# Ten instead of five groups of modulation weights beside the first projection, six instead of eleven in attention

## The chip, the cores and the metric

One core of one Trainium2 chip runs the whole kernel. The metric is the device time of one execution in microseconds (us). Three executions of the kernel before took 3576.84, 3581.84 and 3585.43 us, median 3581.84 us.

## What is computed

Two transformer blocks in a row on 256 tokens of width 2048. The edit lies in the first block, whose modulation vector is a matrix-vector product with a matrix of 2048 x 12288:

```python
mod = jax.nn.silu(c) @ w_ada[l] + b_ada[l]
shift_m, scale_m, gate_m, shift_f, scale_f, gate_f = jnp.split(mod, 6, axis=-1)
h = modulate(rms_norm(x, pre_norm_mix[l]), shift_m, scale_m)
... = jnp.split(h @ w_in[l], split_at, axis=-1)
o_n, o_m = nsa_mixer(...), moba_mixer(...)
o = jnp.concatenate([o_n, o_m], axis=-1) @ w_o[l]
x = x + gate_m[:, None, :] * rms_norm(o, post_norm_mix[l])
```

shift_m and scale_m are needed before `h @ w_in`; gate_m, shift_f, scale_f and gate_f only after `@ w_o`. The first two are a third of the columns of `w_ada`.

## The kernel before

**Groups and steps.** Every large matrix is streamed from memory in groups of 512 columns (GC) and steps of 512 rows (four k-tiles of 128, STEP_K), so one step is one load of 1 MiB. For a projection (`kind` "lin") a step goes through a ring of four slots `raw`: SyncE loads it (L495), ScalarE copies it to `wH` (L568), VectorE subtracts to get `wL` (`split`, L941), and TensorE multiplies with both (L1687 in `layer`, L1645 in `layer_t`), 48 matmuls of 128x256 a step in `layer`. `wH` and `wL` have two buffers: the split of step l waits until TensorE has ended step l-2. `step_done` counts the ended steps.

**Modulation groups.** `w_ada` has 24 groups. A group is not multiplied on TensorE but summed on VectorE: `ada_step` runs four operations of 128x512 for each of its four steps (L1082 for the first two of a group, L1086 for the others) into two partial sums, counted by `ada_sum`. Then `ada_total` on TensorE adds over the partitions with matmuls against a column of ones (L1608, 16 records a group) and counts `ada_rows`; it waits until all 16 operations of its group are counted.

**Where they run.** Groups 0 to 7 run ahead of everything (`ada_a`), through `raw`. Then comes the projection `w_in` with 11 groups of four steps. Beside it run SIDE = 5 groups through a store of their own, `side` (four slots of 1 MiB) with the sums in `side_acc`: SyncE issues a side load (L502) directly behind the raw load of the same step, in each second group of `w_in` (r == 1), after the old contents of the slot were summed. On VectorE `layer` calls `beside_w_in` behind each split from group 1 on; it does the four sums at steps (r, s) = (1,2), (1,3), (2,0), (2,1). On TensorE `ada_total` follows step (2,2). `w_in` runs as one group ahead of a loop (`over_groups` with first = 1) and five turns of two groups, r = 1 and 2; only SyncE's program counts from r = 0 (first = 0).

**The attention stage.** The remaining 11 groups (`ada_b`) go through `raw` again, which is free between the last step of `w_in` and the first of `w_o`. VectorE sums one before the rotary embedding, one before the compressed scores, and then ADA_BESIDE[b] groups in turn b of the loop over eight score blocks: `mask_max(b + 1)` (L1177 or L1183 first), `weights_of(b)`, the ada groups, and the low half of an output (L1224) where a block ends one. TensorE's program for turn b is the scores of b+1 (L1775, L1780, L1783), the totals of the turn before, the transposes of b (they wait for GpSimd's L1529), and the values of b. The loads of `w_o` are issued when all modulation groups are summed (`ada_sum`); ahead of the first split of `w_o` VectorE computes the modulation and its coefficients (L1228 to L1233).

## Time and profile before

| | |
|---|---|
| median of three runs | 3581.84 us |
| the profiled execution | 3579.93 us |
| its span, first to last instruction | 3577.8 us |
| TensorE matmul busy | 3175.6 us, 89% |
| VectorE busy | 1757.8 us, 49% |
| ScalarE busy | 1277.1 us, 36% |
| mean granted clock of TensorE | 0.921 |
| read from memory | 581.99 MB, mean 164 GB/s |

All times of the trace are microseconds from the first instruction. The granted clock is TensorE's, as a share of 2.4 GHz; 0.50 is 1.2 GHz. Matmuls overlap, so the duration of one record (0.28 us for 256 columns) is more than its distance to the next (0.12 us at full clock). In brackets behind a timeline row stands the idle time of the engine just before it and what ended it.

### The profile page before, as it was taken

Reading aid. Unit: us, or ns where it says so; the run is one execution under the profiler, and the core shown is the slowest. Engines: PE = TensorE matmul, PEld = TensorE weight load, DVE = VectorE, ACT = ScalarE, POOL = GpSimd, SP = SyncE. Lnnn points to the kernel's source line nnn. Section 1 sums busy time; section 2 is a strip of 40 time slices with the busy share of each in tenths; the row PEclk is TensorE's granted clock in tenths of the full one; section 3 lists DMA queues with packets and bytes.
Section 4 is the critical chain, followed back from the end, with each engine's and each line's share of the span. In section 5 each row is a group of like instructions: output and inputs, shape, how many; then the busy total and the mean of one; then the engine's idle time right before and its main releaser. Section 6 shows DMA issues by size and latency. Waiting matters only on the chain.

```text
span 3577.8 us, 49987 instructions
## 1 busy us (share of the span) xinstructions
PE 3175.6 (89%) x20990; PEld 2895.5 (81%) x20990; DVE 1757.8 (49%) x1499; ACT 1277.1 (36%) x1117; POOL 139.0 (4%) x105
## 2 busy tenths in 40 slices
PE   3699866989999999899976777799999899999998
PEld 3699655779888997699965666699997798889977
DVE  7655779454443444544335554234364544434444
ACT  1333122344433443333342332144333444334433
POOL 0000201000000000000003222000000000000000
PEclk6799876989999999999978887799999999999999
DMA  9777456645555555545510000255554455555553
GB/s 368 245 266 269 155 205 218 209 132 178 175 188 177 182 172 180 169 157 184 181 53 7 3 3 0 83 182 182 191 179 159 133 184 176 187 175 179 176 179 127
DMA packets 298809, 587.98 MB, mean 164 GB/s; under 512 B 11840, under 2 KB 17472, under 8 KB 298432
## 3 DMA queue, kind: packets, MB, share of 16 engines
q1 hardware_dynamic: 296176, 581.87, 49.0%
q10 hardware_dynamic: 2512, 4.36, 0.5%
q8 instruction: 93, 1.52, 0.2%
q14 instruction: 28, 0.23, 0.0%
HBM read 581.99 MB, written 4.19 MB: 164 GB/s over the span
## 4 chain that ended last, share of the span: by engine, by line
PE 82%; DVE 9%; ACT 3%; issue 3%; DMA 2%; POOL 0%; SPq 0%; DVEq 0%; ACTq 0%
PE ps L1687 44%; PE ps L1645 25%; PE ps L1917 3%; DMA raw<-w_ada 2%; PE ps L2074 2%; DVE ada_acc L1086 1%; DVE wL L941 1%; ACT wH L568 1%; PE ps L1961 1%; PE ps L1950 1%; DVE sq L1039 0%; PE ps L1713 0%; PE ps L1952 0%; PE ps L1738 0%; PE ps L1967 0%
## 5 line engine op out<-in xcount | busy, mean ns | idle before, releaser
L941 DVE TENSOR_TENSOR wL<-raw,wH 128x2048 fp32r<-128x2048 f32 x448 | 1026.6, 2292 | 1428.8 <-ACT wH L568 1424.0
L568 ACT ACTIVATE wH<-raw 128x2048 fp32r<-128x2048 f32 x448 | 857.4, 1914 | 1585.8 <-PE ps L1687 903.1
L1687 PE MATMUL ps<-actH,wH 128*128 128x256 f32 x4352 | 1240.5, 285 | 65.0 <-DVE wL L941 40.8
L1687 PE MATMUL ps<-actL,wH 128*128 128x256 f32 x4352 | 1238.3, 285 | 0.0
L1687 PE MATMUL ps<-actH,wL 128*128 128x256 f32 x4352 | 1237.9, 284 | 0.0
L1687 PEld LDWEIGHTS ps<-actH,wH 128*128 128x128 f32 x4352 | 842.7, 194 | 68.9 <-issue 55.1
L1687 PEld LDWEIGHTS ps<-actL,wH 128*128 128x128 f32 x4352 | 843.0, 194 | 0.0
L1687 PEld LDWEIGHTS ps<-actH,wL 128*128 128x128 f32 x4352 | 842.5, 194 | 0.0
L1645 PE MATMUL ps<-wH,hidH 128*128 128x512 f32 x1024 | 409.2, 400 | 13.0 <-ACT hid_sq L608 11.9
L1645 PE MATMUL ps<-wL,hidH 128*128 128x512 f32 x1024 | 407.6, 398 | 0.0
L1645 PE MATMUL ps<-wH,hidL 128*128 128x512 f32 x1024 | 407.6, 398 | 0.0
L1645 PEld LDWEIGHTS ps<-wH,hidH 128*128 128x128 f32 x1024 | 194.0, 189 | 62.2 <-ACT hid_sq L608 12.7
L1645 PEld LDWEIGHTS ps<-wL,hidH 128*128 128x128 f32 x1024 | 194.1, 190 | 47.5 <-issue 0.5
L1645 PEld LDWEIGHTS ps<-wH,hidL 128*128 128x128 f32 x1024 | 193.9, 189 | 47.4
L1086 DVE SCALAR_TENSOR_TENSOR ada_acc<-raw,csig,ada_acc 128x512 f32<-128x512 f32 x266 | 190.3, 782 | 4.6 <-DMA raw<-w_ada 4.6
L1645 PE MATMUL ps<-wH,actH 128*128 128x512 f32 x256 | 103.3, 403 | 17.4 <-DVE wL L941 17.4
L1608 PE MATMUL ps<-common,ada_acc 128*128 128x1 f32 x304 | 51.1, 298 | 57.8 <-DVE ada_acc L1086 57.7
L1645 PE MATMUL ps<-wL,actH 128*128 128x512 f32 x256 | 101.8, 398 | 0.0
L1645 PE MATMUL ps<-wH,actL 128*128 128x512 f32 x256 | 101.5, 397 | 0.0
L1608 PEld LDWEIGHTS ps<-common,ada_acc 128*128 128x128 f32 x304 | 50.8, 259 | 60.7 <-issue 52.1
L2074 PE MATMUL ps<-yH,wH 128*128 128x256 f32 x256 | 73.6, 288 | 6.9 <-DVE wL L941 6.9
L2074 PE MATMUL ps<-yL,wH 128*128 128x256 f32 x256 | 73.3, 286 | 0.0
(354 smaller groups left out, 2647.0 us busy)
## 6 DMA issues: line engine op xcount, KB each, us to landing
raw<-w_in SPq DMA_DIRECT2D x96, 1024.0 KB, 5.1
raw<-w_ada SPq DMA_DIRECT2D x76, 1024.0 KB, 6.9
raw<-w_up SPq DMA_DIRECT2D x64, 1024.0 KB, 5.2
raw<-w_down SPq DMA_DIRECT2D x64, 1024.0 KB, 5.1
raw<-w_mlp_up SPq DMA_DIRECT2D x64, 1024.0 KB, 5.3
raw<-w_mlp_down SPq DMA_DIRECT2D x64, 1024.0 KB, 5.1
raw<-w_gates SPq DMA_DIRECT2D x48, 1024.0 KB, 5.2
side<-w_ada SPq DMA_DIRECT2D x20, 1024.0 KB, 7.4
```

The lines of the kernel that those rows point to most:

```text
L568: nc.scalar.activation(wH[:, s % SPLIT if L[name]["spg"] > 1 else r % SPLIT, :, :], raw[:, slot, :, :], ACT.Copy).then_inc(wh_ready, 1)
L941: nc.vector.tensor_tensor(wL[:, b, :, :], raw[:, slot, :, :], wH[:, b, :, :].bitcast(F32), ALU.subtract).then_inc(wl_ready, 1)
L1086: ins = nc.vector.scalar_tensor_tensor(sums[:, n % 2, :], w[:, k, :], csig[:, n:n + 1], sums[:, n % 2, :], ALU.mult, ALU.add)
L1608: ins = nc.tensor.matmul(ps[:, bank, bass.ds(n + g * GT + i * (GT * per), 1)], sums[:, j, n * P:(n + 1) * P], ones[:, 0:1], start=(n == 0 ...
L1645: ins = nc.tensor.matmul(ps[:, acc(name, r) + t, :], v[:, kk, ts], w[:, b, k, :], start=(kk == 0 and j == 0), stop=(kk == STEP_K * spg - 1 ...
L1687: ins = nc.tensor.matmul(out, w[:, b, k, cols], v[:, kk, :], start=(kk == 0 and j == 0 and n % 2 == 0), stop=(kk == STEP_K * spg - 1 and j ...
L1917: ins = nc.tensor.matmul(ps[:, out + f, m % 4 * P:(m % 4 + 1) * P], lhs[:, m, :], rhs_[:, m, :], start=(m % 4 == 0), stop=True, skip_group ...
L1950: nc.tensor.matmul(out, AR[hh][:, j, t, 0, :], ST[:, j, hh * RHEAD:(hh + 1) * RHEAD], start=(h == 0), stop=False, skip_group_check=True)
L1961: ins = nc.tensor.matmul(ps[:, 1, h * RHEAD:(h + 1) * RHEAD], Ym[:, 2 * h + t, :], rhs[:, h * RHEAD:(h + 1) * RHEAD], start=(h == 0), stop ...
L2074: ins = nc.tensor.matmul(out, w[:, b, k, cols], v[:, k0 + k, :], start=(start and k == 0 and j == 0 and m % 2 == 0), stop=(stop and k == S ...
```

## The change

SIDE becomes 10. SyncE's program for `w_in` takes the same shape as the others (first = 1), and a side load follows every raw load from group 1 on. VectorE sums step s of side group r-1 directly behind the split of step s of group r, in both groups of a turn, and waits for the total of the side group before at s = 0. TensorE's total comes behind step 2 of every group from group 1 on. In the attention stage ADA_BEFORE stays (1, 1) and ADA_BESIDE becomes (1, 0, 1, 0, 1, 0, 1, 0), so that `ada_b` has six groups.

```diff
--- before.py
+++ after.py
@@ -39,7 +39,7 @@
 GC = 512
 GT = GC // P
 RAW, SPLIT = 4, 2
-SIDE = 5
+SIDE = 10
 
 
 CMP_LEN, CMP_STRIDE = 32, 16
@@ -455,7 +455,7 @@
         out_of = [g for g, n in ((0, 3), (1, 3), (2, 1), (3, 1)) for _ in range(n)]
         NSUB = len(subs)
 
-        ADA_BEFORE, ADA_BESIDE = (1, 1), (2, 1, 1, 1, 1, 1, 1, 1)
+        ADA_BEFORE, ADA_BESIDE = (1, 1), (1, 0, 1, 0, 1, 0, 1, 0)
         assert len(ADA_BESIDE) == NSUB and sum(ADA_BEFORE + ADA_BESIDE) == 16 - SIDE
         rope_pairs = [QN, QN + 2, QN + 4, QN + 6, KC, KS, KW] + list(range(QM, VM, 2))
         v_pairs = [VS, VW] + list(range(VM, PROJ1, 2))
@@ -495,19 +495,19 @@
                         sp.dma_start(raw[:, slot, :, :],
                                      w[:, k0 + s * STEP_K:k0 + (s + 1) * STEP_K, bass.ds(n0 + r * GC + i * (U * GC), GC)]
                                      ).then_inc(raw_in[slot], 16)
-                        if name == "w_in" and r == 1:
-
-                            side_g = L["ada_a"]["groups"]
-                            sp.wait_ge(ada_sum, STEP_K * (4 * side_g + s + 1) + i * (4 * STEP_K))
+                        if name == "w_in" and not (isinstance(i, int) and r == 0):
+
+                            side_g = L["ada_a"]["groups"] + r - 1
+                            sp.wait_ge(ada_sum, STEP_K * (4 * side_g + s + 1) + i * (8 * STEP_K))
                             sp.dma_start(side[:, s, :, :], w_ada[:, s * STEP_K:(s + 1) * STEP_K,
-                                                                 bass.ds(side_g * GC + i * GC, GC)]).then_inc(side_in[s], 16)
+                                                                 bass.ds(side_g * GC + i * (2 * GC), GC)]).then_inc(side_in[s], 16)
 
                 if l["kind"] == "ada":
                     if l["l0"]:
                         sp.wait_ge(wl_ready, RAW + l["l0"])
                 elif l["a0"]:
                     sp.wait_ge(ada_sum, STEP_K * (RAW + l["a0"]))
-                over_groups(sp, name, 0, body)
+                over_groups(sp, name, int(name == "w_in"), body)
 
             stream("ada_a")
             sp.dma_start(c1[:, :], a["c1"]).then_inc(c1_in, 16)
@@ -1096,14 +1096,11 @@
 
             def beside_w_in(i, r, s):
 
-                s_ = 4 * (r - 1) + s - 2
-                if not 0 <= s_ < 4:
-                    return
-                g = L["ada_a"]["groups"]
-                if s_ == 0:
-                    dve.wait_ge(ada_rows, 2 + g + i)
-                dve.wait_ge(side_in[s_], 16 + i * 16)
-                ada_step(g, s_, side[:, s_, :, :], side_acc, i, 1)
+                g = L["ada_a"]["groups"] + r - 1
+                if s == 0:
+                    dve.wait_ge(ada_rows, 2 + g + i * 2)
+                dve.wait_ge(side_in[s], 16 * r + i * 32)
+                ada_step(g, s, side[:, s, :, :], side_acc, i, 2)
 
             def ada_raw(g):
 
@@ -1688,8 +1685,8 @@
                                                            start=(kk == 0 and j == 0 and n % 2 == 0),
                                                            stop=(kk == STEP_K * spg - 1 and j == 2), skip_group_check=True)
                         ins.then_inc(step_done, 1)
-                        if name == "w_in" and r == 2 and s == 2:
-                            ada_total(L["ada_a"]["groups"], i, 1, side_acc, 6)
+                        if name == "w_in" and not (isinstance(i, int) and r == 0) and s == 2:
+                            ada_total(L["ada_a"]["groups"] + r - 1, i, 2, side_acc, 6)
                         if turn is not None and isinstance(i, int) and i == 0 and r == 0 and s == 0:
                             turned(turn, ((2, 0), (2, 1), (3, 0), (3, 1)))
```

## Rows read from the trace of the kernel before

**Rows 1.** The page: chain that ended last, by line

```profile
PE ps L1687 44%; PE ps L1645 25%; PE ps L1917 3%; DMA raw<-w_ada 2%; PE ps L2074 2%; DVE ada_acc L1086 1%; DVE wL L941 1%; ACT wH L568 1%; PE ps L1961 1%; PE ps L1950 1%; DVE sq L1039 0%; PE ps L1713 0%; PE ps L1952 0%; PE ps L1738 0%; PE ps L1967 0%
```

**Rows 2.** Windows: us; busy (count) per engine; PEclk, DMA share, GB/s

```profile
126.00:391.00 265.00, 264.78 (x2192) 264.81 (x2193) 149.53 (x126) 89.52 (x52) 0.00 (x0) 0.99 0.72 248
223.00:246.00 23.00, 23.00 (x195) 23.00 (x194) 12.81 (x10) 8.43 (x5) 0.00 (x0) 1.00 1.02 364
541.00:592.00 51.00, 34.89 (x170) 29.59 (x169) 46.72 (x77) 13.98 (x46) 7.39 (x6) 0.67 0.69 250
```

**Rows 3.** Chain in order of time, first projection: start, us, what

```profile
192.25 1.68 PE ps L1608 x16
193.93 46.18 PE ps L1687 x384
```

**Rows 4.** Timeline in w_in, VectorE, ScalarE, TensorE: start, us, what [idle before]

```profile
171.20 2.29 DVE L941 TENSOR_TENSOR wL<-raw,wH 128x2048 fp32r<-128x2048 f32 x1 [0.82 <-ACT wH L568]
173.40 2.73 DVE L1086 SCALAR_TENSOR_TENSOR side_acc<-side,csig,side_acc 128x512 f32<-128x512 f32 x4
...
169.25 1.92 ACT L568 ACTIVATE wH<-raw 128x2048 fp32r<-128x2048 f32 x1 [3.85 <-PE ps L1687]
175.01 1.91 ACT L568 ACTIVATE wH<-raw 128x2048 fp32r<-128x2048 f32 x1 [3.84 <-PE ps L1687]
192.29 1.91 ACT L568 ACTIVATE wH<-raw 128x2048 fp32r<-128x2048 f32 x1 [3.85 <-PE ps L1687]
199.83 1.91 ACT L568 ACTIVATE wH<-raw 128x2048 fp32r<-128x2048 f32 x1 [5.63 <-PE ps L1687]
...
192.09 1.84 PE L1608 MATMUL ps<-common,side_acc 128*128 128x1 f32 x16
```

**Rows 5.** TensorE timeline at stops, then windows around them and 500 us

```profile
942.88 0.50 PE L1645 MATMUL ps<-wH,hidH 128*128 128x512 f32 x1 [2.97 <-ACT hid_sq L608]
...
1532.51 0.39 PE L1687 MATMUL ps<-actH,wH 128*128 128x256 f32 x1 [2.01 <-DVE actL L1047]
...
1128.40:1131.70 3.30, 3.30 (x18) 3.30 (x17) 0.55 (x1) 0.00 (x0) 0.00 (x0) 0.51 0.45 99
1533.30:1536.60 3.30, 3.30 (x30) 3.30 (x29) 3.08 (x4) 2.54 (x2) 0.00 (x0) 1.00 0.00 0
3377.80:3381.10 3.30, 3.30 (x16) 2.66 (x15) 0.00 (x0) 0.14 (x1) 0.00 (x0) 1.00 0.75 263
...
500.30:503.70 3.40, 0.16 (x2) 0.08 (x1) 3.40 (x7) 0.00 (x0) 0.00 (x0) 0.51 1.04 380
```

**Rows 6.** Timeline of the attention stage, VectorE and TensorE

```profile
485.96 10.99 DVE L1086 SCALAR_TENSOR_TENSOR ada_acc<-raw,csig,ada_acc 128x512 f32<-128x512 f32 x14
497.67 9.35 DVE L1086 SCALAR_TENSOR_TENSOR ada_acc<-raw,csig,ada_acc 128x512 f32<-128x512 f32 x14
506.94 0.33 DVE L1177 TENSOR_TENSOR pcmp<-ps,c 128x60 f32<-128x60 f32 x2
560.32 0.35 DVE L1177 TENSOR_TENSOR pcmp<-ps,c 128x60 f32<-128x60 f32 x2 [1.70 <-PE ps L1775]
574.25 0.69 DVE L1183 TENSOR_TENSOR probs<-ps,common 128x512 f32<-128x512 f32 x1
592.69 0.69 DVE L1183 TENSOR_TENSOR probs<-ps,common 128x512 f32<-128x512 f32 x1 [2.03 <-PE ps L1783]
...
496.69 1.99 PE L1775 MATMUL ps<-kcT,proj 128*128 128x15 f32 x16
498.54 1.93 PE L1608 MATMUL ps<-common,ada_acc 128*128 128x1 f32 x16
```

**Rows 7.** Timeline around the first load of w_o: SyncE, VectorE, TensorE

```profile
624.76 12.67 SPq L495 DMA_DIRECT2D raw<-w_o  x6
...
625.03 1.23 DVE L1224 TENSOR_TENSOR actL<-ps,actH 128x1024 fp32r<-128x1024 f32 x1 [0.59 <-ACT actH L761]
...
634.39 0.77 PE L1645 MATMUL ps<-wH,actH 128*128 128x512 f32 x1 [7.95 <-DVE wL L941]
```

## The prediction

> **What bounds the kernel now.** I read the chain of work that ended last first: TensorE leads it, with 44% of the span in the projection matmuls of L1687 and 25% in those of L1645 [rows 1]. Then the stages by window [rows 2]: in the first projection (126 to 391 us) TensorE is busy all the time at a granted clock of 0.99, VectorE 56% and ScalarE 34% of it; in the middle of the attention stage (541 to 592) TensorE is busy 68% at a clock of 0.67, and VectorE 92%. So the edit moves work out of a stage in which TensorE waits, often beside a busy VectorE, into one in which it never waits. Third, the chain inside the projection [rows 3]: behind each total it has 46.18 us of matmuls (two groups, eight steps, 5.76 us a step by the spacing of ScalarE's rows in [rows 4]) then 1.68 us of the next ada_total, five times. No wait lies between. Last, who is late in attention [rows 6] and where w_o begins [rows 7].
>
> **What moves.** Five more groups of modulation weights are loaded, summed and totalled beside w_in (ten instead of five), and five fewer in the attention stage (one instead of two at b=0, none at b=1, 3, 5, 7). Nothing else changes in amount: sixteen remain behind ada_a. The placing changes too. Today the four sums of a side group lie at steps (1,2), (1,3), (2,0), (2,1) and its total follows step (2,2), one step after the last sum was issued. In the changed kernel sum s follows the split of step s of the same group, and the total still follows step s=2. The PE program therefore asks for sum 3, which VectorE issues only after the split of step 3.
>
> **Part 1, five more totals on TensorE.** Each is 16 records. In a group with a total ScalarE's next split comes 7.54 us after the last instead of 5.76 (192.29 and 199.83 in [rows 4]), so one total costs 1.78 us, and TensorE has nothing to hide it under. 5 x 1.78 = 8.9 us.
>
> **Part 2, the new wait before each of ten totals.** One step with a side sum, from [rows 4]: ScalarE's split starts at 169.25, which is when step l-2 ended; VectorE's split starts at 171.20, its sums run from 173.40 to 176.13; ScalarE's next split at 175.01 marks the end of step l-1. The total after step l-1 wants exactly the sum that ends at 176.13. TensorE can issue the total some 0.2 us before the end of the step is signalled (L1608 starts at 192.09, ScalarE is released at 192.29), so it stands from 174.81 to about 176.18: 1.37 us. Bounds: 1.1 us (signal to signal) and 1.5 us (if VectorE's start drifts by its 0.1 us). Ten totals: 13.7 us (11 to 15). Behind that wait on TensorE's queue stands step 3 of the group, whose weights are ready since 173.40, so all of it is lost. VectorE itself keeps up: 2.2 + 2.73 us of work in 5.76, with 0.82 us idle before each split [rows 4]; its wait on ada_rows at s=0 comes after a split, some 1 us after the total has ended. ScalarE gets nothing new.
>
> **Part 3, the clock.** Stop and total together keep the dense matmuls away for 1.37 + 1.78 = 3.15 us, ten times. What the rows show of such pauses [rows 5]: TensorE stops for 2.97 us at six seams between feed-forward layers (942.88 is the first), and behind five of them the granted clock is 0.50 or 0.51 (1.2 instead of 2.4 GHz) for a stretch of some 3.4 us (1128.40 is one), then 1.00 again; the sixth (3377.80) shows 1.00. Two stops of 2.01 us (one ends at 1532.51) show 1.00 behind them, as do today's five totals of 1.78 us. That totals count as good as nothing for the clock is seen at 498.54 [rows 6]: 15-column matmuls and one total from 496.69 to 500.47 without a stop, and the next stretch, from 500.30, is at 0.51. So 3.15 us lies just beyond the pause that cost the clock five times in six; I take nine of ten. A stretch at half clock holds about 12 fewer 256-column matmuls (x18 against x30 [rows 5]) of 0.12 us: 1.5 us. 9 x 1.5 = 13.5 us, bounds 0 (none falls) and 18 (all fall, some into a second stretch).
>
> The Trainium skill, "TensorE: Matmul & The Clock Gate", section "Why this matters for your kernels", says that mid-kernel drops come from idle gaps of more than about 3 us between bursts. Taken literally it speaks against these falls, as the idle part here is 1.4 us and the totals are matmuls: the stage would then grow by the first two parts alone. The row at 498.54 speaks against that reading; the case has a rival of its own below.
>
> **Part 4, transfers.** A step now always brings two 1 MiB loads. Today that holds in every second group, where 364 GB/s flow for 23 us and nothing is late (window 223 to 246 in [rows 2]). The 8.39 MB of a group take 23.0 us at that rate against 24.8 us of TensorE without the stop and 26.2 with it. A load is issued four steps (23 us) ahead of its use. On SyncE's queue the load of the next step stands behind each side load's wait for the old sum of its slot; that sum directly follows the split which frees slot s, and the next load needs the split after it, so nothing is held. Cost 0; without that cover a group would grow only by what exceeds 24.8 us.
>
> **Part 5, the attention stage.** At b=0 VectorE sums two groups, 484.38 to 507.02, and mask_max(2) (L1177) starts at 506.94 although its scores stood at 498.55 (PE, L1775) and the first group ended at 496.95 [rows 6]. With one group it starts at about 498.6: 8.3 us gained. What is late next is TensorE's scores. At b=1 the group goes as well, but the next mask waited for TensorE's scores anyway, as those behind b=3 (560.32, 1.70 us idle) and b=5 (592.69, 2.03 us) did [rows 6]: these three groups were hidden and their removal gives 0. Only at 574.25 were sums and scores late together, and that group (b=4) stays. At b=7 the sums end at 624.4, only then the loads of w_o go out (624.76), and TensorE starts w_o at 634.39 [rows 7]. Without this group the loads go out about 15 us earlier; next late are the last output and its low part (625.03 + 1.23), the modulation and coefficient rows up to 627.18 and one split of 2.29 us: start at 629.5, 4.9 us gained. Totals in this stage lay in TensorE's waits. Sum 13.2 us. The bounds come from the clock: one turn of this loop takes 13.9 us (560.32 to 574.25) and the next 18.4 us (574.25 to 592.69), the clock having a large part in it, and shifted work can draw either; 13.2 give or take 4.5 us.
>
> **Sum.** +8.9 + 13.7 + 13.5 - 13.2 = +22.9 us. The profiled execution took 3579.93 us (span 3577.8 and 2.1 around it), which gives 3602.8; the median of the three runs lies 1.9 us above it: **3604.7 us**, 0.64% slower.
>
> **Rivals.**
> - *The clock holds*, since TensorE truly idles only 1.37 us at a time: parts 1, 2 and 5, +22.6 - 13.2 = +9.4: 3591 us. For it: the stop proper is below the 2.01 us that cost nothing. Against: the weak matmuls at 498.54 and the five falls. (This is what the Trainium skill's rule above comes to.)
> - *The total finds its sum ready.* If VectorE's sum of step 3 ended 1.4 us earlier than the rows of step-by-step timing let me place it, only the five totals remain: +8.9 - 13.2 = -4.3: 3577.5 us, no change that can be told. Against: the order of the program and three rows of [rows 4] that agree.
> - *Attention is bound by VectorE* (the other side). VectorE sums in 10.1 us alone and 12.5 us beside GpSimd [rows 6], and fills most of the stage [rows 2]. If each group taken out shortens the stage by its whole length, 5 x 11.3 = 56 us go, less the 36 us of parts 1 to 3: 3562 us. It decides from the point where the masks find their scores waiting instead of the reverse; of the three masks in [rows 6] with full scores behind a sum, two waited for their scores.
>
> **How the numbers follow.** Forecast 0.62, clock holds 0.22, sum ready 0.09, attention bound 0.04, 0.03 for something costlier than all (loads that fall behind). The forecast's own range is 3596 to 3614 (part 3 from 7 to 18 us, part 5 within its bounds). The range of 3586 to 3614 adds most of the second case and leaves out the others. A measurement of this kernel can tell about 0.2% (7 us) from no change. Slower by more: 0.62, three quarters of 0.22, and 0.03: 0.81. Within: a quarter of 0.22 and 0.09: 0.15. Faster: 0.04.
>
> **What would show it.** In the chain between 126 us and the end of w_in the pieces of L1687 should shrink from 46.18 to about 23 us (longer where the clock fell), each followed by a VectorE piece of ada sums near 1.3 us and 1.7 us of L1608, ten times; w_in should end near 427 us instead of 391. L1608 should show idle time ended by VectorE (today none in this stage), and windows of some 3.4 us behind the totals a granted clock of 0.5; a stage at 0.99 says that the clock held. VectorE's row of splits should wait for ScalarE, never the reverse. In attention mask_max(2) should start directly behind L1775, and w_o some 5 us after the last output's low part begins. If the span from the end of w_in to the first w_o matmul shrinks by much more than 13 us, part 5 is wrong; if L1608 does not wait, part 2 is.

## The result, and the profile after

| | before | after |
|---|---|---|
| median (lowest to highest) | 3580.81 us (3576.84 to 3585.43, six runs) | 3597.61 us (3595.14 to 3598.55, six runs) |
| ratio to before, 95% interval | | 1.0044 [1.0031, 1.0057] |
| profiled execution, its span | 3579.93, 3577.8 us | 3595.55, 3593.5 us |
| mean granted clock | 0.921 | 0.922 |

The change costs 16.8 us by the medians, 0.44%. That is slower, inside the range of 3586 to 3614, and 7 us below the point that was forecast.

The span can be cut at landmarks that both kernels have: the first matmul of w_in, the first of the attention stage, the first of w_o, the last load of the second w_in, the first load of the recurrence's weights, the first load of the stage behind it, the end. The landmarks are rows of the timelines; this table takes them from one trace of each execution, in us. All kernels of the experiments are in it.

| trace | w_in | attention | w_o to last w_in2 load | to recurrence | four recurrence turns | rest | span |
|---|---|---|---|---|---|---|---|
| before | 264.9 | 243.3 | 1163.0 | 101.6 | 398.2 | 1280.6 | 3577.8 |
| before, second trace | 264.2 | 246.6 | 1164.8 | 102.1 | 383.9 | 1282.0 | 3570.9 |
| before, third trace | 265.0 | 246.8 | 1163.0 | 101.6 | 398.3 | 1280.6 | 3581.5 |
| after | 308.4 | 226.9 | 1164.2 | 102.2 | 383.9 | 1281.9 | 3593.5 |
| after, second trace | 309.0 | 227.7 | 1164.2 | 102.2 | 394.4 | 1281.7 | 3606.0 |
| e1_total_late | 273.1 | 228.3 | 1164.1 | 102.2 | 383.9 | 1281.9 | 3560.9 |
| e2_split_pause | 288.6 | 229.9 | 1164.2 | 102.1 | 384.0 | 1281.9 | 3577.7 |
| e3_attention_alone | 263.8 | 229.8 | 1164.1 | 102.1 | 398.7 | 1280.6 | 3565.2 |
| e5_second_at_b0 | 272.5 | 238.1 | 1163.7 | 102.2 | 383.9 | 1281.9 | 3569.1 |
| e6_last_at_b7 | 272.5 | 230.1 | 1164.9 | 102.2 | 394.5 | 1281.7 | 3571.4 |
| e7_before_three_ahead | 265.1 | 240.4 | 1162.8 | 101.6 | 398.2 | 1280.7 | 3574.9 |
| e8_three_ahead_early_w_o | 263.8 | 234.0 | 1163.2 | 102.1 | 383.8 | 1282.1 | 3555.2 |
| e9_early_w_o | 264.4 | 241.4 | 1163.4 | 102.2 | 383.7 | 1282.1 | 3563.1 |

Read it column by column. w_in is 264 to 265 us in every trace of before and 308 to 309 in both of after: +44. Attention is 243 to 247 against 227 to 228: -16 to -20. In the recurrence no instruction differs between the kernels, and yet its four turns take either 384 or 394 to 399 us, in traces of one and the same kernel: a difference in that column can't be credited to the change from one trace of each.

First, w_in. The windows of the profile after, as in [rows 2] (us; busy and count of TensorE, its weight loads, VectorE, ScalarE and GpSimd; granted clock, DMA share, GB/s):

```profile
126.00:424.00 298.00, 286.11 (x2208) 284.12 (x2208) 198.34 (x203) 89.51 (x52) 0.00 (x0) 0.92 0.80 282
223.00:246.00 23.00, 21.68 (x169) 21.49 (x168) 15.17 (x16) 6.65 (x4) 0.00 (x0) 0.93 0.82 287
541.00:592.00 51.00, 33.55 (x152) 28.32 (x151) 23.61 (x48) 13.98 (x46) 6.67 (x6) 0.63 0.37 134
```

The clock of the stage is 0.92 where it was 0.99, TensorE is no longer busy throughout, and in the third window VectorE is busy 23.6 us of 51 where it was 46.7 (the same times, but the attention stage begins 43 us later now, so that this is another part of it). The chain in order of time (start, us, what), as in [rows 3]:

```profile
199.05 1.94 PE ps L1605 x16
200.99 24.63 PE ps L1684 x192
225.67 0.36 issue
226.03 0.76 DVE side_acc L1086
226.78 0.14 issue
226.92 1.94 PE ps L1605 x16
228.86 18.89 PE ps L1684 x144
```

L1605 is the total and L1684 the matmuls of `layer` in the changed file. One group now stands between two totals, and VectorE's last sum is a link of the chain. TensorE's waits from 126 to 425 us, which hold nine of the ten (line waited for: us in total, times, longest; the tenth total starts at 425.25 behind 1.3 us as well) and the timeline of VectorE and ScalarE beside one total, as in [rows 4]:

```profile
PE ps L1605 <- DVE side_acc L1086: 11.8, 9, 1.3
```

```profile
166.77 2.73 DVE L1086 SCALAR_TENSOR_TENSOR side_acc<-side,csig,side_acc 128x512 f32<-128x512 f32 x4
...
168.37 1.91 ACT L568 ACTIVATE wH<-raw 128x2048 fp32r<-128x2048 f32 x1 [3.84 <-PE ps L1684]
```

The four operations of the sum begin at 166.77 and end at 169.50; the end of the step is signalled at 168.37; the total starts at 169.65. The windows behind two of the totals, at 169.65 and at 226.92:

```profile
171.65:175.05 3.40, 3.40 (x17) 3.40 (x17) 3.07 (x5) 0.00 (x0) 0.00 (x0) 0.50 0.97 345
175.05:178.45 3.40, 3.40 (x20) 3.40 (x19) 0.00 (x0) 0.00 (x0) 0.00 (x0) 0.58 1.02 378
178.45:181.85 3.40, 3.40 (x30) 3.40 (x30) 0.00 (x0) 1.35 (x1) 0.00 (x0) 1.00 0.54 206
...
228.92:232.32 3.40, 3.40 (x18) 3.40 (x18) 3.08 (x5) 0.00 (x0) 0.00 (x0) 0.53 1.02 337
232.32:235.72 3.40, 3.40 (x30) 3.40 (x29) 0.00 (x0) 0.00 (x0) 0.00 (x0) 0.97 1.04 385
```

Behind all ten totals the clock fell from 2.4 to 1.2 GHz: seven times as behind the one at 226.92, for about one such stretch, and three times as behind the one at 169.65, for nearly two. Counted against the 30 or 31 matmuls of a stretch at full clock, 12 or 13 are missing each of the seven times and 22 to 24 each of the three. The second trace of after shows the same: ten falls behind ten totals, seven short and three long.

Second, attention. VectorE's timeline of after, the rows that answer to [rows 6] and the last ones before w_o:

```profile
531.86 10.99 DVE L1086 SCALAR_TENSOR_TENSOR ada_acc<-raw,csig,ada_acc 128x512 f32<-128x512 f32 x14
544.76 0.35 DVE L1174 TENSOR_TENSOR pcmp<-ps,c 128x60 f32<-128x60 f32 x2 [1.91 <-PE ps L1772]
...
560.29 0.69 DVE L1180 TENSOR_TENSOR probs<-ps,common 128x512 f32<-128x512 f32 x1 [14.09 <-PE ps L1780]
...
596.30 0.35 DVE L1174 TENSOR_TENSOR pcmp<-ps,c 128x60 f32<-128x60 f32 x2 [13.80 <-PE ps L1772]
...
610.24 0.69 DVE L1180 TENSOR_TENSOR probs<-ps,common 128x512 f32<-128x512 f32 x1
...
628.32 0.69 DVE L1180 TENSOR_TENSOR probs<-ps,common 128x512 f32<-128x512 f32 x1 [3.14 <-PE ps L1780]
...
657.05 1.23 DVE L1221 TENSOR_TENSOR actL<-ps,actH 128x1024 fp32r<-128x1024 f32 x1 [10.64 <-ACT actH L761]
658.90 4.49 DVE L941 TENSOR_TENSOR wL<-raw,wH 128x2048 fp32r<-128x2048 f32 x2
```

Every mask but the one at 610.24 now waits for TensorE's scores, for some 14 us in two of the turns that have lost their sums (560.29, 596.30); in the third, before 628.32, the wait falls into two parts around an L1221. The split of w_o at 658.90 follows the coefficients without a wait. To see which part gained, I cut the stage once more, at the starts of two of VectorE's masks: the second of the eight masks of the stage (525.97 in after, 480.07 in before; between it and the next lie the sums of b=0) and the last (628.32 and 592.69).

| trace | start to second mask | to last mask | to w_o |
|---|---|---|---|
| before, three traces | 89.0, 91.6, 92.6 | 112.6, 112.7, 112.6 | 41.7, 42.3, 41.6 |
| after, two traces | 91.6, 92.6 | 102.4, 102.1 | 33.0, 33.0 |
| e1_total_late | 93.2 | 102.0 | 33.1 |
| e2_split_pause | 94.5 | 102.4 | 33.0 |
| e3_attention_alone | 94.4 | 102.3 | 33.1 |
| e5_second_at_b0 | 89.0 | 113.1 | 36.0 |
| e6_last_at_b7 | 89.1 | 102.0 | 39.0 |
| e7_before_three_ahead | 95.9 | 102.7 | 41.7 |
| e8_three_ahead_early_w_o | 94.3 | 102.7 | 37.0 |
| e9_early_w_o | 91.6 | 112.9 | 37.0 |

The first column wanders by some 5 us where the work is the same (89.0 to 92.6 among traces of before, 94.5 in e2), and the granted clock wanders with it: up to the first mask it is 0.81 in the first trace of before and 0.76 in e3. The other two repeat to within 1 us. So the edit gained 10.3 us in the middle and 8.7 at the end of the stage, 19.0 in all; against the first trace of before 2.6 of it was lost again by the first column's chance.

### The profile page after: what moved, and what is told of

Read it like the earlier page. It is cut to its first block, busy times and chain, and to the rows that moved or that the text cites. A ratio compares the mean times of both kernels' runs of the same rounds, so it can differ in the third digit from the quotient of the medians.

```text
span 3593.5 us, 50063 instructions
## 1 busy us (share of the span) xinstructions
PE 3177.2 (88%) x20990; PEld 2898.4 (81%) x20990; DVE 1751.0 (49%) x1499; ACT 1276.9 (36%) x1117; POOL 137.6 (4%) x105
## 4 chain that ended last, share of the span: by engine, by line
PE 81%; DVE 9%; ACT 4%; issue 3%; DMA 2%; POOL 0%; SPq 0%; DVEq 0%; ACTq 0%
PE ps L1684 44%; PE ps L1642 25%; PE ps L1914 3%; DMA raw<-w_ada 2%; PE ps L2071 2%; ACT wH L568 1%; DVE wL L941 1%; DVE ada_acc L1086 1%; PE ps L1605 1%; PE ps L1958 1%; PE ps L1710 0%; PE ps L1947 0%; DVE sq L1039 0%; PE ps L1735 0%; PE ps L1949 0%
## 5 line engine op out<-in xcount | busy, mean ns | idle before, releaser
L1684 PE MATMUL ps<-actH,wH 128*128 128x256 f32 x4352 | 1250.1, 287 | 64.2 <-DVE wL L941 39.6
L1684 PE MATMUL ps<-actL,wH 128*128 128x256 f32 x4352 | 1247.0, 287 | 0.0
L1684 PE MATMUL ps<-actH,wL 128*128 128x256 f32 x4352 | 1246.6, 286 | 0.0
L1684 PEld LDWEIGHTS ps<-actH,wH 128*128 128x128 f32 x4352 | 852.6, 196 | 68.3 <-issue 54.5
L1684 PEld LDWEIGHTS ps<-actL,wH 128*128 128x128 f32 x4352 | 852.3, 196 | 0.0
L1684 PEld LDWEIGHTS ps<-actH,wL 128*128 128x128 f32 x4352 | 851.6, 196 | 0.0
L1086 DVE SCALAR_TENSOR_TENSOR ada_acc<-raw,csig,ada_acc 128x512 f32<-128x512 f32 x196 | 138.7, 775 | 5.0 <-DMA raw<-w_ada 5.0
L1642 PE MATMUL ps<-wH,actH 128*128 128x512 f32 x256 | 102.8, 402 | 14.8 <-DVE wL L941 14.8
L1086 DVE SCALAR_TENSOR_TENSOR side_acc<-side,csig,side_acc 128x512 f32<-128x512 f32 x140 | 96.1, 746 | 0.0
L1605 PE MATMUL ps<-common,ada_acc 128*128 128x1 f32 x224 | 40.9, 312 | 54.5 <-DVE ada_acc L1086 54.5
L1605 PEld LDWEIGHTS ps<-common,ada_acc 128*128 128x128 f32 x224 | 40.5, 278 | 56.8 <-issue 53.4
```

What stands on the lines that cost most here:

```text
L1086: ins = nc.vector.scalar_tensor_tensor(sums[:, n % 2, :], w[:, k, :], csig[:, n:n + 1], sums[:, n % 2, :], ALU.mult, ALU.add)
L1605: ins = nc.tensor.matmul(ps[:, bank, bass.ds(n + g * GT + i * (GT * per), 1)], sums[:, j, n * P:(n + 1) * P], ones[:, 0:1], start=(n == 0 ...
L1642: ins = nc.tensor.matmul(ps[:, acc(name, r) + t, :], v[:, kk, ts], w[:, b, k, :], start=(kk == 0 and j == 0), stop=(kk == STEP_K * spg - 1 ...
L1684: ins = nc.tensor.matmul(out, w[:, b, k, cols], v[:, kk, :], start=(kk == 0 and j == 0 and n % 2 == 0), stop=(kk == STEP_K * spg - 1 and j ...
```

## The experiments

My theory is the forecast's: the change costs three things in w_in (totals, stop, clock) and returns two in attention (the second group at b=0, the group ahead of w_o). The rivals stand in the prediction.

### The total one step later

In the changed kernel the total of a group follows its step 3 instead of step 2, so that its last sum has ended.

```diff
-                        if name == "w_in" and not (isinstance(i, int) and r == 0) and s == 2:
+                        if name == "w_in" and not (isinstance(i, int) and r == 0) and s == 3:
                             ada_total(L["ada_a"]["groups"] + r - 1, i, 2, side_acc, 6)
```

> The changed kernel with the total of a side group behind step 3 instead of step 2 of its projection group; all else, also the sums, as in the changed kernel. Theory (the wait for the fourth sum and the half-clock stretches behind it are 35 of the 43.3 us by which the first projection grew): L1605 never idles in this stage, the stage from its first matmul (about 126 us) to the first gate matmul takes 265.1 + 8.9 = 274 us instead of 308.4, its clock is 0.99, and the whole kernel takes 3597.6 - 34.4 = 3563 us, below the kernel before. Rival 1 (the two 1 MiB loads of every step, now in all groups, hold the stage back): the stage stays near 300 us and TensorE waits for VectorE's splits. Rival 2 (VectorE cannot carry a split and four sums in every step, and its wait for the old total at s = 0, now 3.4 us long, pushes the splits late): gaps of 1 to 3 us before L1684 once a group, stage 284 to 300 us.

Measured: 3570.22 us (3557.77 to 3576.68, ten runs) against 3581.1, ratio 0.9969 [0.9955, 0.9982]. The stage came out as expected, the median 7 us above the expected 3563; the ten runs spread over 19 us, with a mean granted clock of 0.929 in the shortest and 0.922 in the longest, and the traced one took 3562.96. Its window over w_in and VectorE's wait in it:

```profile
127.00:399.00 272.00, 271.62 (x2259) 271.65 (x2259) 199.85 (x205) 89.52 (x52) 0.00 (x0) 0.99 0.89 316
```

```profile
DVE side_acc L1082 <- PE ps L1605: 29.6, 9, 3.3
```

TensorE is busy all the time again at 0.99, and the stage is 273.1 us: 8.2 more than before for five more totals, 35.3 less than the changed kernel. The wait has not gone, it changed sides: VectorE now waits 3.3 us for the total before it may overwrite `side_acc`, which costs nothing because it has that slack. The same ten groups with the same loads, placed one step later, beat the kernel before, by its medians and also trace against trace with like recurrence turns (3562.96 against 3572.98). The loss of the change is its placing, not its amount.

### The stop without the total

The wait stays behind step 2, the total goes behind step 3. This takes the two halves of the pause apart. (STEP_K is 4; the wait is the one that the total itself had.)

```diff
+                        if name == "w_in" and not (isinstance(i, int) and r == 0) and s == 2:
+                            pe.wait_ge(ada_sum, STEP_K * (RAW + 4 * (L["ada_a"]["groups"] + r)) + i * (STEP_K * 8))
-                        if name == "w_in" and not (isinstance(i, int) and r == 0) and s == 2:
+                        if name == "w_in" and not (isinstance(i, int) and r == 0) and s == 3:
                             ada_total(L["ada_a"]["groups"] + r - 1, i, 2, side_acc, 6)
```

> As the changed kernel, but TensorE only waits for the fourth sum behind step 2 and does the total behind step 3. The stop and the total are both there ten times and 5.8 us of dense matmuls lie between them. Theory (a stop of 1.3 us and a total of 1.8 us cost the clock only when they stand together): no half-clock stretch in the first projection, stage 265.1 + 8.9 + 13.5 = 287.5 us, kernel about 3577 us. Rival (the stop alone brings the clock down): granted clock again near 0.92 and the stage near 305 us. Rival (the wait itself is not what costs, only the total's place): the stage as short as with the late total alone, 274 us.

Measured: 3578.3 us (3576.88 to 3590.09, ten runs), ratio 0.9999 [0.9989, 1.0009]. Window over w_in, TensorE's wait from 126 to 400 us, and the chain beside one stop:

```profile
127.00:415.00 288.00, 274.99 (x2267) 273.03 (x2267) 199.49 (x204) 90.35 (x53) 0.00 (x0) 0.99 0.84 302
```

```profile
PE ps L1684 <- DVE side_acc L1086: 11.7, 9, 1.3
```

```profile
169.91 0.75 DVE side_acc L1086
170.66 0.12 issue
170.78 6.01 PE ps L1684 x48
176.79 1.68 PE ps L1605 x16
178.47 3.58 PE ps L1684 x29
```

The stops are as long as in the changed kernel, 1.3 us, the totals as many, but 6.0 us of matmuls lie between, and the clock stays at 0.99. This splits the stage: e2 less e1 is the stop, 288.6 - 273.1 = 15.5 us, and the changed kernel less e2 is the clock, 308.4 - 288.6 = 19.8 us. Neither a 1.3 us stop nor a 1.7 us total brought the clock down by itself; one right behind the other did ten times in ten, in each of the two traces of after.

### The attention stage alone

The kernel before with six ada_b groups and nothing added beside w_in. Five modulation groups are left out: the last 20 columns of the modulation take their bias alone.

```diff
-              ("ada_b", "ada", 16 - SIDE, 4), ("w_o", "lin", 4, 4),
+              ("ada_b", "ada", 6, 4), ("w_o", "lin", 4, 4),
...
-        ADA_BEFORE, ADA_BESIDE = (1, 1), (2, 1, 1, 1, 1, 1, 1, 1)
+        ADA_BEFORE, ADA_BESIDE = (1, 1), (1, 0, 1, 0, 1, 0, 1, 0)
...
```

> The kernel before with six instead of eleven groups in the attention stage and nothing added beside the first projection: five groups of modulation weights are left out altogether (the last 20 columns of the modulation take the bias alone), so its time holds only the relief of the attention stage. Theory: only the second group at b=0 (8.3 us) and the gate that the group of b=7 puts before the loads of w_o (4.9 us) count, plus or minus the clock: 243.4 us from the first gate matmul to the first matmul of w_o become 227 to 230, kernel 3564 to 3568 us. Rival (VectorE bound, each group counts): 243.4 - 56 = 187 us, kernel about 3525 us. Rival (the 16.5 us that the changed kernel's stage lost are partly the clock's luck): 235 us and a kernel near 3573 us.

Measured: 3566.31 us (3562.63 to 3567.3, five runs), ratio 0.9963 [0.9949, 0.9977]: 14.8 us by the medians. In the table of the stage it has the middle and the end of the changed kernel (102.3 and 33.1), 19 us less than before, and a first column 1.8 us longer than the longest of before. Nothing of 56 us, which VectorE's rival named, is there.

### The kernel before and the changed kernel once more

No edit; each was traced again, before twice and after once, to see what two traces of one kernel differ by.

> The kernel before once more, unchanged, for its profile. In the profiled executions the four recurrence turns (from the last load of lw to the first load of the gates' weights) took 224.7 us before and 210.1 us in the changed kernel, with the same instructions and with 37 us at half clock in 2150 to 2200 us against 10 us. Theory (chance: where the half-clock stretches fall differs from one execution to the next): another execution of the kernel before gives another time for these turns, anywhere from 208 to 226 us. Rival (the turns are slower in this kernel for a reason of its own): 224.7 us again within 2 us.

> The kernel before once more, for a third trace: the four recurrence turns at either about 384 or about 398 us, w_in at 264 to 265, attention at 243 to 247. If the long turns belong to the kernel before, 398; if they are a chance, either.

> The changed kernel once more, for a second trace. If the 383.9 against 398.2 us of the four recurrence turns is a chance of the execution and not of the kernel, this trace may show either; if it belongs to the changed kernel, 384 again. The stage of w_in is expected at 305 to 311 us in either case, with the clock fallen behind all ten totals, the attention stage at 225 to 231.

Measured: before 3572.98 and 3583.6 us, after 3607.99 us. Windows over the four recurrence turns: the first of the kernel before, then its second trace, then the second trace of the changed kernel:

```profile
1899.00:2297.20 398.20, 298.19 (x1968) 253.44 (x1968) 201.65 (x284) 106.16 (x177) 95.05 (x67) 0.81 0.01 3
```

```profile
1905.00:2288.90 383.90, 280.55 (x1968) 237.89 (x1968) 201.70 (x284) 106.08 (x177) 95.10 (x68) 0.86 0.01 4
```

```profile
1929.90:2324.30 394.40, 291.01 (x1968) 246.63 (x1968) 201.57 (x284) 106.09 (x177) 95.00 (x67) 0.84 0.01 3
```

The same 1968 matmuls, the same VectorE and ScalarE times, and a granted clock of 0.81, 0.86 or 0.84. Most of it lies in one place, here in the kernel before and in its second trace:

```profile
2150.00:2200.00 50.00, 38.12 (x210) 31.23 (x209) 17.04 (x22) 12.45 (x22) 5.98 (x6) 0.63 0.00 0
```

```profile
2156.00:2206.00 50.00, 34.23 (x247) 26.80 (x245) 24.76 (x31) 15.09 (x26) 6.69 (x6) 0.90 0.00 0
```

So the 14.3 us by which the first profile of after seems to win in the recurrence can't be put down to the edit: before shows both times, and after two of its own. Compared with like turns, the change costs 3595.55 - 3572.98 = 22.6 us (both short) and 3607.99 - 3583.6 = 24.4 us or 3607.99 - 3579.93 = 28.1 us (both long, though of 394 against 398). The 16.8 us of the medians are smaller. The six runs of after lie within 3.4 us of its short trace, and the median of before lies by its long ones, so before seems to draw long turns more often. Only profiled executions show their turns, so this stays an inference, but the mean granted clock, which is known of every execution, bears it out. The short trace of before has 0.924, its long ones 0.920 and 0.921; of 53 other executions of before, made beside the experiments, 43 lie at 0.922 or below and took at least 3577.3 us, and ten at 0.923 or above, none of them longer than that. The six runs of after lie at 0.921 and 0.922, as its short trace (0.922), where its long one has 0.919. What decides the draw is open. The time at which the stage begins doesn't do it alone: the turns begin at 1895.1 us in e1 and at 1895.2 in e6, and take 383.9 and 394.5. One profile of each kernel would have credited the edit with it.

### The second group at b=0, and the last group at b=7

Both are the kernel with the late total; only the place of the six groups differs.

```diff
-        ADA_BEFORE, ADA_BESIDE = (1, 1), (1, 0, 1, 0, 1, 0, 1, 0)
+        ADA_BEFORE, ADA_BESIDE = (1, 1), (2, 0, 1, 0, 1, 0, 0, 0)
```

> The kernel with the late total (e1), but its second ada_b group of the loop summed at b=0 instead of b=6: two groups at b=0, one at b=2 and b=4, none after. Read by the stage from the first gate matmul to the first matmul of w_o, 228.3 us in e1. Theory (a second group at b=0 holds back mask_max(2), all others are hidden): 8.3 to 9.2 us more, 237 us. Rival (VectorE bound, only the number of groups counts): 228 us as in e1, since six groups are six groups. Rival (the gain came from the loads of w_o alone): 228 us or less, as these go out even earlier.

Measured: 3573.29 us (3571.18 to 3580.46, eight runs), ratio 0.998 [0.9969, 0.999]. The stage is 9.8 us longer with the same number of groups; the middle column alone grew by 11.1 us, from 102.0 to 113.1, which is that of before with all its eleven groups. What costs in this stage is the second group at b=0, not how many there are.

```diff
-        ADA_BEFORE, ADA_BESIDE = (1, 1), (1, 0, 1, 0, 1, 0, 1, 0)
+        ADA_BEFORE, ADA_BESIDE = (1, 1), (1, 0, 1, 0, 1, 0, 0, 1)
```

> The kernel with the late total (e1), with the group of b=6 summed at b=7 instead. Theory (the group of b=7 is hidden itself but holds back the loads of w_o): the loads go out about 0.3 us after the sums of b=7 and the stage from gates to w_o takes 4.9 us more than e1's 228.3, 233 us; up to 237 if the clock at the last values falls as in the kernel before. Rival (the whole group counts): 240 us. Rival (nothing, the split is late anyway): 228 us.

Measured: 3573.59 us (3569.1 to 3576.44, eight runs), ratio 0.9982 [0.997, 0.9994]. The stage grew by 1.8 us only, and by that the expectation failed. The timelines of VectorE, ScalarE and SyncE ahead of w_o show why the stage is the wrong measure:

```profile
620.77 0.17 DVE L1230 TENSOR_TENSOR coef<-mod,vecs 128x16 f32<-128x16 f32 x1
623.68 1.91 ACT L568 ACTIVATE wH<-raw 128x2048 fp32r<-128x2048 f32 x1 [5.37 <-DMA raw<-w_o]
625.67 2.29 DVE L941 TENSOR_TENSOR wL<-raw,wH 128x2048 fp32r<-128x2048 f32 x1 [4.74 <-issue]
```

```profile
618.48 28.21 SPq L495 DMA_DIRECT2D raw<-w_o  x8
```

The gate is there with its full price: the loads go out at 618.48, when the last sums have ended, ScalarE waits for the first of them until 623.68, and VectorE's split stands 4.74 us in all. The end of the stage grew by 5.9 us (33.1 to 39.0); the first column, ahead of any difference between the two kernels in this stage, was 4.1 us shorter by chance.

### Three groups ahead, and early loads of w_o

What the theory offers for the kernel before, without the ten totals: the second group of b=0 goes ahead of the compressed scores.

```diff
-        ADA_BEFORE, ADA_BESIDE = (1, 1), (2, 1, 1, 1, 1, 1, 1, 1)
+        ADA_BEFORE, ADA_BESIDE = (1, 2), (1, 1, 1, 1, 1, 1, 1, 1)
```

> The kernel before (five groups beside the first projection, eleven after it) with two groups instead of one ahead of the compressed scores, where VectorE stood idle for 11.0 us, and one instead of two at b=0. Theory (only the second group at b=0 was in the way): the stage from gates to w_o falls from 243.3 and 246.6 us (two executions) by 8 us, less up to 1.5 us for a total that now waits for sums, 236 to 239 us; kernel about 3574 us. Rival (what the extra group needs, its loads, come too late at that place, and it holds back the compressed scores): no gain, 245 us.

Measured: 3574.61 us (3566.95 to 3577.68, ten runs), ratio 0.9983 [0.9973, 0.9993]. The middle fell to 102.7 as it should. The stage, at 240.4 us, missed the expected 236 to 239, since the first column is 95.9, 3 us above the longest of before. Whether the group ahead costs anything there isn't shown. TensorE's longest wait for VectorE in this part is 5.8 us in both kernels; e8, with the same group ahead, has 94.3 in the column, and e3, without it, 94.4; and the granted clock up to the first mask is 0.76 in e7 as in e3.

Then one change more, alone on the kernel before and on top of the three groups ahead: each of the first four loads of w_o waits for the sums of its own slot instead of all sums.

```diff
+                        if name == "w_o" and isinstance(i, int) and i == 0 and r == 0:
+                            sp.wait_ge(ada_sum, STEP_K * (l["a0"] + s + 1))
...
-                elif l["a0"]:
+                elif l["a0"] and name != "w_o":
                     sp.wait_ge(ada_sum, STEP_K * (RAW + l["a0"]))
-                over_groups(sp, name, 0, body)
+                over_groups(sp, name, int(name == "w_o"), body)
```

> The kernel before with one change: each of the first four loads of w_o waits for the modulation sums of its own slot only, not for all sums of the stage, so that three of four steps lie ready when VectorE ends its last group. The theory (part 5 of the prediction: at the end of the attention stage the loads of w_o, then the modulation rows and the split, are late one after the other) expects the first matmul of w_o about 4.9 us earlier: stage from the first gate matmul to the first w_o matmul 238 to 242 us (243.3 and 246.6 in the two traces of the kernel before), ratio 0.9986. The rival, that the last group's place is worth only the 1.8 us which moving it back behind the last block cost in the run before, expects 242 to 245 us, ratio 0.9995. The recurrence turns are expected at either about 384 or about 398 us, as by chance.

Measured: 3564.92 us (3563.08 to 3567.07, five runs) against 3580.11, ratio 0.9961 [0.9947, 0.9975]. SyncE's first loads of w_o, and VectorE ahead of it:

```profile
618.58 15.59 SPq L497 DMA_DIRECT2D raw<-w_o  x6
```

```profile
627.11 1.22 DVE L1226 TENSOR_TENSOR actL<-ps,actH 128x1024 fp32r<-128x1024 f32 x1 [0.61 <-ACT actH L763]
...
629.28 4.49 DVE L943 TENSOR_TENSOR wL<-raw,wH 128x2048 fp32r<-128x2048 f32 x2
```

The loads go out 8.5 us before the last low part instead of beside it, the split no longer waits, and the end of the stage is 37.0 us instead of 41.7: 4.7 us, as the theory had it (4.9). The median gained 15 us, three times that. The trace has the short recurrence turns, which before's median has not, so some 10 us of the ratio may not belong to the edit; five runs within 4 us of each other suggest that this kernel draws them often.

> As e7, and the first four loads of w_o each wait only for the sums of their own slot instead of for all modulation sums. No load and no sum is moved to the first projection. Theory: the stage from gates to w_o loses 4.9 us more, 231 to 234 us, within some 4 us of what the six groups reach, at no cost in the first projection (264.5 us): kernel about 3568 us, below the kernel before, the changed kernel and e1. Rival (the split of w_o waits for the sums, totals and coefficients anyway): no further gain, 236 to 239 us.

Measured: 3557.99 us (3555.87 to 3559.92, four runs), ratio 0.9938 [0.992, 0.9957]. It beats both kernels, with 102.7 and 37.0 us in the two columns, 14.6 us less there than before, while the first column, 94.3, lies within what it wanders by; and again it has the short turns. By the whole attention stage 9 to 13 us of the 23 are the edits' (234.0 against 243.3 to 246.8).

## Why the prediction was right, step by step

The forecast was 22.9 us more than the profiled execution of before. With like recurrence turns it is 22.6 to 28.1. The sum held in part by luck: w_in grew by 7.4 us more than forecast and attention gave back 5.8 us more, and the two errors lean against each other. The median came out 7 us below the point, most likely because before's median has long turns in it and that of after short ones, which the forecast didn't know of.

| step | forecast | measured | from |
|---|---|---|---|
| part 1, five totals | +8.9 | +8.2 | w_in of e1 less before |
| part 2, the stop | +13.7 (11 to 15) | +15.5 | e2 less e1 |
| part 3, the clock | +13.5 (0 to 18) | +19.8 | after less e2 |
| part 4, transfers | 0 | 0 | no wait for a transfer in w_in |
| part 5, second group at b=0 | -8.3 | -10.3 | middle column |
| part 5, end of the stage | -4.9 | -8.7 | last column |
| sum | +22.9 | +24.5 | |

**Part 1** was right in mechanism and size.

**Part 2** was right in mechanism. The stop itself is 1.3 us, ten times, against 1.37 forecast. The rest of the 15.5 us, some 2.4, is time at the edges of the stops that I hadn't counted. Idle time runs from the end of the last matmul's record, which is 0.28 us long, while the next one would have started 0.12 us after its start: 0.16 us of overlap is lost. And TensorE's first matmul behind a stop has 0.38 us where the others have 0.28. Ten times 1.31 + 0.16 + 0.10 is 15.7 us.

**Part 3** was right in kind and too small. I took nine falls of 1.5 us; there were ten, and three of them lasted nearly twice as long. By the missing matmuls (seven times 12 or 13, three times 22 to 24, of 0.12 us each) the price is 19 us, which agrees with the 19.8 between the kernels. The step that failed is "a stretch at half clock holds about 12 fewer 256-column matmuls": true of one stretch, but the rows at 1128.40 in [rows 5] showed a fall that ended after one, and I took its length for all. The upper bound of 18 us was crossed by 1.8. The rival in which the clock holds is refuted ten times in ten, and e2 says under what condition it would have been true. The Trainium skill, "TensorE: Matmul & The Clock Gate", section "Why this matters for your kernels", puts the risk with idle gaps of more than about 3 us, as the prediction cited. Read as idle time alone, the trace doesn't agree: the longest idle time here is 1.3 us, and matmuls of one column right behind it didn't keep the clock. Read as the distance between two stretches of dense matmuls, it does: 3.2 us in the chain of after (225.67 to 228.86). Two stops of 2.01 and 2.25 us, shown next, cost the clock too, which the page's 3 us doesn't cover.

The prediction also took too much from two stops of 2.01 us that didn't cost the clock. The second of them did cost it in another trace of the same kernel, and a stop of 2.25 us, which it hadn't listed, cost it in the first. The windows behind the 2.25 us and the second 2.01 us in the first trace of before, then behind the second in its second trace:

```profile
759.60:763.00 3.40, 3.40 (x16) 3.40 (x17) 3.40 (x6) 1.61 (x2) 0.00 (x0) 0.53 0.02 5
2819.28:2822.68 3.40, 3.40 (x28) 3.40 (x29) 3.40 (x6) 1.85 (x2) 0.00 (x0) 1.00 0.00 0
```

```profile
2810.45:2813.85 3.40, 3.40 (x17) 3.40 (x18) 3.40 (x6) 1.86 (x2) 0.00 (x0) 0.57 0.00 0
```

The thirteen traces all have these three stops: the clock fell behind the one of 2.25 us in ten of them, behind the second of 2.01 us in nine, and behind the first of 2.01 us in none. So these rows don't show that a pause below 3 us is free, as the prediction took it. A total without a stop, 1.5 us between dense matmuls, was free ten times in e1.

**Part 4** held: the loads of e1's w_in come to 316 GB/s on average and no matmul waits.

**Part 5** was right in its places and too small in both. The middle gained 10.3 us instead of 8.3: the mask behind b=0 starts 12.9 us after its sums begin instead of 21.0 (531.86 and 544.76 against 485.96 and 506.94), 8.1 us where 8.3 were forecast. The other 2 us are spread over the next turns: 1.1 before the mask behind b=1, and 0.4 before each of those behind b=2, 3 and 5. In b=3 and b=5 GpSimd's work is 0.36 us shorter (below). In b=2 it is as long as it was, and TensorE's scores ahead of the mask took 2.99 us instead of 3.38. The end gained 8.7. The first matmul of w_o starts 4.3 us behind the last low part instead of 9.4, a gain of 5.1 (4.7 by e9 and e8), which is the gate on the loads with its 4.9. The other 3.6 is that the last low part starts 28.7 us behind the last mask (628.32 and 657.05) instead of 32.3 (592.69 [rows 6] and 625.03 [rows 7]). It isn't the sums that were taken away: e5 has none at all there, and its last low part starts 31.7 us behind the mask (601.44 and 633.15). What goes with it is the clock, as the windows of the two last turns show, of before, after and e5:

```profile
592.70:610.70 18.00, 11.24 (x54) 9.77 (x53) 16.78 (x24) 6.15 (x19) 3.22 (x2) 0.62 0.54 196
610.70:625.70 15.00, 9.70 (x46) 8.46 (x45) 14.38 (x20) 2.54 (x3) 3.22 (x2) 0.66 0.23 84
```

```profile
628.30:645.30 17.00, 5.96 (x31) 5.20 (x31) 16.88 (x24) 6.15 (x19) 3.22 (x2) 0.79 0.00 0
645.30:657.10 11.80, 8.50 (x43) 7.64 (x43) 1.13 (x4) 2.62 (x4) 2.89 (x2) 0.71 0.93 336
```

```profile
601.40:618.40 17.00, 8.28 (x28) 6.89 (x28) 4.08 (x7) 5.73 (x19) 2.89 (x2) 0.60 0.00 0
618.40:634.40 16.00, 7.80 (x28) 6.60 (x28) 2.76 (x5) 4.24 (x5) 2.89 (x2) 0.68 0.00 0
```

The shorter one has 0.79 and 0.71, the longer ones 0.60 to 0.68. This is no draw: in the five traces with the six groups of after (after twice, e1, e2, e3) the last low part comes 28.7 us behind the last mask at a mean clock of 0.76, in the six with a group in each of the last turns (before three times, e7, e8, e9) 32.3 us at 0.63. It goes with the placing; by what way isn't shown. I had kept the clock's part out of the term and in its bounds of 4.5 us, which 19.0 oversteps by 1.3. That three of the five groups were nearly hidden is confirmed by e5, which has as few groups as after and the middle of before.

**The other rivals.** "The total finds its sum ready" fell with the ten waits of L1605. Its time is what e1 builds: 8.2 - 19.0 = -10.8 us by the stages. That its medians gave -10.9 is partly chance, as recurrence turns of both sorts are mixed in them. "Attention is bound by VectorE" fell with e3.

## What to carry to other kernels

Before moving work beside a dense matmul stage, place the instruction that consumes it one step behind the producer's last part: here the same ten groups cost 27 us more or less in time by one step of placing (3597.6 against 3570.2 by the medians; w_in alone 35.3). Count a wait and the small matmuls behind it as one pause, since the clock did. And take a second trace of the same kernel before a stage that the edit doesn't touch is given a reason.

## What the hardware showed that I had not expected

- **Stop and total cost the clock only together.** A stop of 1.3 us with 6.0 us of matmuls ahead of the total left the granted clock at 0.99 (e2), a total of 1.7 us alone too (e1); a stop of 1.3 us and the total directly behind it brought 1.2 GHz in ten of ten in each of two traces, for about 3.4 us seven times and about twice that three times.
- **One program, different times.** The four recurrence turns took 383.7 to 384.0 us in seven traces and 394.4 to 398.7 in six, with the same instructions; the granted clock there was 0.86 in the one sort and 0.81 or 0.84 in the other. The Trainium skill, "TensorE: Matmul & The Clock Gate", section "What's actually happening", says that where the clock rises varies between runs of one kernel; the traces of before agree, and here it is worth up to 15 us, 0.4%.
- **GpSimd and VectorE slow each other.** The same pair of GpSimd operations took 3.25 us where VectorE's sums lay beside it and 2.89 where they didn't:

```profile
546.22 3.25 POOL L1529 TENSOR_TENSOR probs<-probs,rsum 128x512 f32<-128x512 f32 x2 [16.55 <-DVE rsum L1211]
```

```profile
582.57 2.89 POOL L1526 TENSOR_TENSOR probs<-probs,rsum 128x512 f32<-128x512 f32 x2 [16.17 <-DVE rsum L1208]
```

The first row is of before, the second of after, both in the turn b=3. VectorE's fourteen sums tell the same from their side, 9.35 us alone and 10.99 beside GpSimd [rows 6]; the difference lies in one operation, which takes 2.38 us there instead of 0.74. The masks wait for GpSimd's work by way of TensorE's transposes, so a sum that was hidden still cost 0.4 us in this turn and in b=5. The Trainium skill, "GPSIMD Engine Reference", section "Specifications", says that the two share their interfaces to the on-chip memory; the trace agrees and gives the sizes.
